# Scores in three rounded passes, and five pieces of work moved between points, in a 1-core fp32 layer stack

## The reference, cut to what matters

```python
# first layer: attention of each head, q and k 64 wide
s = jnp.einsum('bdhnqe,bdhnke->bdhnqk', qb, kb)      # three dilations, masked
...
y_att = o_att * jax.nn.silu(ag.astype(f32))
y = jnp.concatenate([y_att, y_hg], axis=-1).astype(h.dtype) @ w_out
h = h + rmsnorm(y, g_post)
gate = jax.nn.sigmoid((h @ w_pg).astype(f32))
...
# layers two and three: differential attention, two 64-wide halves of a head
qb = lax.dynamic_slice_in_dim(q, i * Q_BLOCK, Q_BLOCK, axis=1)
s = jnp.einsum('bqhcd,bkhcd->bhcqk', qb, k).astype(jnp.float32)
s = jnp.where(kpos[None, :] <= qpos[:, None], s, -jnp.inf)
p = jax.nn.softmax(s, axis=-1)
w = p[:, :, 0] - lam * p[:, :, 1]
...
ret_out = rms_norm(ro).reshape(B, S, RET_W) * jax.nn.silu(rg)
```

## Time and profile before

| | us |
|---|---|
| median of 3 runs | 3032.59 (3032.46 to 3035.77) |
| the profiled execution | 3033.25 |
| its span in the trace | 3031.2 |
| PE busy | 2968.0 (98%) |
| DVE, ACT, POOL busy | 1616.7, 1304.1, 1351.8 |
| mean granted PE clock | 0.994 |

### The profile page before, as it was taken

The page is one execution under the profiler, slowest core; times in us unless marked ns, Lnnn a source line. Parts: engine busy times, 40 slices in busy tenths (PEclk is TensorE's granted clock), DMA queues, the critical chain, the costliest instruction groups (busy, mean ns, idle before and its releaser), DMA issues. The chain is left out here.

```text
span 3031.2 us, 48608 instructions
## 1 busy us (share of the span) xinstructions
PE 2968.0 (98%) x17338; PEld 2407.8 (79%) x17338; DVE 1616.7 (53%) x2411; ACT 1304.1 (43%) x2552; POOL 1351.8 (45%) x1022
## 2 busy tenths in 40 slices
PE   8999999999999999999999999999999999999998
PEld 6888888877777788878888877788888888777886
DVE  5377666655657306653556575551435565755412
ACT  6545444354556334453333334453533333344532
POOL 4444444443433356454444433344644444433444
PEclk9999999999999999999999999999999999999999
DMA  6322222222222334333322222243343222222433
GB/s 240 107 86 108 83 83 82 72 84 83 81 77 78 131 119 153 104 118 136 118 91 87 91 84 70 77 147 102 121 149 118 91 86 92 84 70 74 149 101 107
DMA packets 79010, 313.30 MB, mean 103 GB/s; under 512 B 7440, under 2 KB 11920, under 8 KB 51472
## 3 DMA queue, kind: packets, MB, share of 16 engines
q1 hardware_dynamic: 54832, 266.62, 26.1%
q10 hardware_dynamic: 24032, 44.76, 4.2%
HBM read 293.01 MB, written 18.35 MB: 103 GB/s over the span
## 5 line engine op out<-in xcount | busy, mean ns | idle before, releaser
L340 POOL TENSOR_TENSOR w_low<-w_raw,w_high 128x512 fp32r<-128x512 f32 x844 | 1136.1, 1351 | 1525.2 <-ACT w_high L851 1502.5
L405 PE MATMUL z<-u_high,w_high 128*128 128x512 f32 x3216 | 1277.4, 397 | 15.3 <-DVE work L1491 14.6
L406 PE MATMUL z<-u_low,w_high 128*128 128x512 f32 x3216 | 1257.9, 391 | 0.0
L851 ACT ACTIVATE w_high<-w_raw 128x512 fp32r<-128x512 f32 x832 | 520.0, 629 | 1112.6 <-PE z L409 1075.9
L409 PE MATMUL z<-u_high,w_low 128*128 128x512 f32 x3216 | 862.3, 390 | 0.0
L405 PEld LDWEIGHTS z<-u_high,w_high 128*128 128x128 f32 x3216 | 605.8, 188 | 165.2 <-issue 32.4
L409 PEld LDWEIGHTS z<-u_high,w_low 128*128 128x128 f32 x3216 | 605.0, 188 | 127.7
L406 PEld LDWEIGHTS z<-u_low,w_high 128*128 128x128 f32 x3216 | 606.3, 189 | 119.7
L1867 DVE TENSOR_TENSOR work<-work 128x512 f32<-128x512 f32 x78 | 90.9, 1165 | 277.5 <-ACT work L1140 264.8
L1491 DVE TENSOR_TENSOR work<-z,work 128x512 f32<-128x512 f32 x110 | 76.1, 692 | 181.9 <-PE z L409 145.3
L363 POOL TENSOR_TENSOR pass_weights<-w_raw,pass_weights 128x512 fp32r<-128x512 f32 x96 | 134.4, 1424 | 62.3 <-ACT pass_weights L1053 61.8
(11 more groups left out here) (341 smaller groups left out, 3698.3 us busy)
## 6 DMA issues: line engine op xcount, KB each, us to landing
w_raw<-in_wt SPq DMA_DIRECT2D x213, 1024.0 KB, 4.9
w_raw<-in_wt SPq DMA_DIRECT2D x144, 256.0 KB, 3.0
out_hT<-work ACTq DMA_DIRECT2D x10, 1024.0 KB, 5.8
work<-out_hT ACTq DMA_DIRECT2D x8, 1024.0 KB, 10.3
work<-in_xT SPq DMA_DIRECT2D x4, 1024.0 KB, 16.5
e_scratch<-work ACTq DMA_DIRECT2D x1, 4096.0 KB, 16.7
work<-in_xT ACTq DMA_DIRECT2D x4, 1024.0 KB, 10.9
mixed<-e_scratch ACTq DMA_DIRECT2D x4, 1024.0 KB, 9.2
```

Source lines behind the costliest of these rows:

```text
L340: pool.tensor_tensor(WL[:, 4 * q:4 * q + 4, :], RAW[:, t.odd, 512 * q:512 * q + 512].rearrange("p (k c) -> p k c", k=4), WH[:, 4 * q:4 * q ...
L405: pe.matmul(bank[:], WH[:, k, :], UH[:, k, :], start=(k == 0), stop=False)
L406: pe.matmul(bank[:], WH[:, k, :], UL[:, k, :], start=False, stop=False)
L851: act.activation(WH[:, 4 * q:4 * q + 4, :], RAW[:, n.odd, 512 * q:512 * q + 512].rearrange("p (k c) -> p k c", k=4), ACT.Copy).then_inc(se ...
```

## The change

1. **Scores.** A head's score matmul becomes three fp32r matmuls (`head_scores`): high by high, high by low, low by high, the two heads in turn. `take_heads` makes the parts: two rounded copies (heads_high, QKH), a drain, and two subtractions (heads_low, QKL).
2. **Rotation.** In the differential steps the first rotation goes from point 6 to point 7, behind `dif_out`.
3. **Roots.** `root_row` and `turn_back` come one region later, and between the first and second layer one (first half) or three (second half) regions later.
4. **Gate tile.** In the R_DIF step the gate's `rstd_mul` and `bounded` are taken at point 11 and only the product at the end; the RG-LRU gate's `rstd_mul` and `bounded` follow right behind the step, its product at point 3 of the next.
5. **Third tile.** After pair step 13 PE runs three quarters of the third output tile (`third_ahead`), ahead of `att_values`. They signal `third_used`, on which ACT waits before it rounds three quarters of the next tile's weights into the same place; the fourth quarter stays in `third_tiles` and frees four at once.

```diff
-            def quarter(t, q, gen=None, spare=None, behind=2):
+            def quarter(t, q, gen=None, spare=None, behind=2, done="w_free", freed=1):
...
-                mm.then_inc(sem("w_free"), 1)
+                mm.then_inc(sem(done), freed)
...
-            def third_tiles(t):
+            def third_tiles(t, ahead=0):
                 for s in range(2):
-                    for q in range(4):
-                        quarter(t.plus(2 + s), q, spare=None if s else OUT_BANK)
+                    for q in range(0 if s else ahead, 4):
+                        quarter(t.plus(2 + s), q, spare=None if s else OUT_BANK, freed=ahead + 1 if ahead and not s else 1)
+            def third_ahead(t, n):
+                pe.wait_ge(sem("sm_done"), PRIMED + 8 * PAIRS)
+                for q in range(n):
+                    quarter(t.plus(2), q, spare=OUT_BANK, done="third_used")
...
+            def head_scores(n, hd, a, w):
+                o = slice(64 * hd, 64 * hd + 64)
+                q, k = ((QKH, QKH), (QKH, QKL), (QKL, QKH))[n]
+                return pe.matmul(SC[hd][:, 0:w], q[o, 0, a * P:(a + 1) * P], k[o, 1, 0:w], start=(n == 0), stop=(n == 2))
...
             def dif_scores(j, a):
-                for hd in range(2):
-                    u = 2 * a + hd
-                    pe.wait_ge(sem("dsm_done"), PRIMED + j * 8 + max(u - 1, 0))
-                    o, w = 64 * hd, (a + 1) * P
-                    pe.matmul(SC[hd][:, 0:w], row(QT)[o:o + 64, a * P:(a + 1) * P], row(KTR)[o:o + 64, 0:w],
-                              start=True, stop=True).then_inc(sem("ds_done"), 1)
+                w = (a + 1) * P
+                for n in range(3):
+                    for hd in range(2):
+                        if n == 0:
+                            pe.wait_ge(sem("dsm_done"), PRIMED + j * 8 + max(2 * a + hd - 1, 0))
+                        mm = head_scores(n, hd, a, w)
+                        if n == 2:
+                            mm.then_inc(sem("ds_done"), 1)
...
                 if pg:
-                    return {6: lambda: root_row(n),
-                            7: lambda: turn_back(n, (sem("pg_prod"), 14 + 2 * h), h, (0, 12), BACK_PG[h])}
-                return {3: lambda: root_row(n),
-                        4: lambda: turn_back(n, (sem("z_free"), t - T_HGG + (5 if h else 2)), h, (12,), BACK)}
+                    return {7 + 2 * h: lambda: root_row(n),
+                            8 + 2 * h: lambda: turn_back(n, (sem("pg_prod"), 14 + 2 * h), h, (0, 12), BACK_PG[h])}
+                return {4: lambda: root_row(n),
+                        5: lambda: turn_back(n, (sem("z_free"), t - T_HGG + (5 if h else 2)), h, (12,), BACK)}
...
                     for q in range(4 if weights else 0):
-                        if region is None:
+                        if ahead and q < 3:
+                            high(tt, q, q + 1, "third_used")
+                        elif region is None:
                             high(tt, q)
...
             def take_heads(done):
                 v.drain()
-                v.tensor_copy(row(QT), row(QN))
-                v.tensor_copy(row(KTR), row(KN)).then_inc(sem(done), 1)
+                for n, x in ((0, QN), (1, KN)):
+                    v.tensor_copy(QKH[:, n, :], row(x))
+                v.drain()
+                for n, x in ((0, QN), (1, KN)):
+                    i = v.tensor_tensor(QKL[:, n, :], row(x), QKH[:, n, :].bitcast(F32), ALU.subtract)
+                i.then_inc(sem(done), 1)
...
-                dif = dict(rot=(CTD, STD, 32), scales=scd, take="dqt_ready", ends=(6, 10), gate_tile_at=2)
+                dif = dict(rot=(CTD, STD, 32), scales=scd, take="dqt_ready", ends=(7, 10), gate_tile_at=2)
                 step(Tile(T_L2 + R_DIF, (PER_LAYER, l)), gate=(gl + 6, 6), work="ret", j=l * RET_HEADS + RET_HEADS - 1, m=5,
-                     **{**dif, "ends": (3, 7)})
+                     **{**dif, "ends": (3, 7), "gate_taken_at": 11})
+                rstd_mul(Tile(T_L2 + R_DIF + 3, (PER_LAYER, l)), row(RW))
+                bounded()
```

More of the change, by code:

```diff
@@ L757, in _, with last_pair @@
                 step(Tile(T_ATT, (4, i)), work="att", j=i - 1, late=i - 2)
-            step(None, work="att", j=PAIRS - 1, late=PAIRS - 2, at=LAST_PAIR, between={p: lambda p=p: pair_step(Tile(T_OUT), p - 1, 1) for p in range(1, 16)})
+            def last_pair(p):
+                pair_step(Tile(T_OUT), p - 1, 1)
+                if p == 14:
+                    third_ahead(Tile(T_OUT), 3)
+            step(None, work="att", j=PAIRS - 1, late=PAIRS - 2, at=LAST_PAIR, between={p: lambda p=p: last_pair(p) for p in range(1, 16)})
             pair_step(Tile(T_OUT), 15, 1)
-            third_tiles(Tile(T_OUT))
+            third_tiles(Tile(T_OUT), 3)
             def tiles_in_pairs(t, a, b):
@@ L1129, in out_slots, with one @@
             def out_slots(t, n, gain, block, loads, region):
-                def one(tt, m, s, used, bank, weights=True, taken=None, region=None):
+                def one(tt, m, s, used, bank, weights=True, taken=None, region=None, ahead=False):
                     for q in range(4 if weights else 0):
-                        if region is None:
+                        if ahead and q < 3:
+                            high(tt, q, q + 1, "third_used")
+                        elif region is None:
                             high(tt, q)
@@ L1146, in out_slots @@
                 for s in range(2):
-                    one(t.plus(2 + s), 2 + s, s, n + s + 1, Z[s] if s else OUT_BANK)
+                    one(t.plus(2 + s), 2 + s, s, n + s + 1, Z[s] if s else OUT_BANK, ahead=block == 1 and s == 0)
                 with act.Fori(2, OUT_FULL // 2 - 1) as i:
@@ L1791, in step @@
                             rstd_mul(t.plus(3), row(VT))
+                    if p == gate_taken_at:
+                        rstd_mul(t.plus(gate_tile_at), row(RW))
+                        bounded()
                     if work is not None:
@@ L1822, in step @@
                         else:
-                            gate_tile(t.plus(gate_tile_at), gate[0], MIX[:, gate[1], :])
+                            if gate_taken_at is None:
+                                rstd_mul(t.plus(gate_tile_at), row(RW))
+                                bounded()
+                            gate_product(gate[0], MIX[:, gate[1], :])
             def hg_col(i):
@@ L1828, in lru_gate, with lru_product @@
             def lru_gate(t, n, b):
-                gate_tile(t, n, row(RW))
+                rstd_mul(t, row(RW))
+                bounded()
+                lru_product(n, b)
+            def lru_product(n, b):
+                gate_product(n, row(RW))
                 v.tensor_tensor(MIX[:, 10 + b, :], MIX[:, 10 + b, :], row(RW), ALU.mult).then_inc(sem("lru_done"), 1)
```

18 lines of the change are left out of this document (10 added, 8 removed).

## The result

| | us |
|---|---|
| before, median of 5 runs | 3032.59 (3031.93 to 3035.77) |
| changed, median of 5 runs | 3017.33 (3014.90 to 3020.64) |
| ratio, with 95% interval | 0.9948 (0.9933 to 0.9962) |
| changed, profiled execution and its span | 3018.78, 3016.8 |
| forecast | 3008 (3000 to 3023) |

The kernel became faster by 15.3 us, 0.5%. The side and the range were right; the gain is 60% of the 25.2 that the sum had. The runs of the changed kernel also lie further apart (5.7 us) than a forecast of single microseconds would like: the slowest of the five had a mean granted clock of 0.993 and the fastest 0.995, and 0.002 of 3017 us is 6.

The account below looks back on a forecast made before the run. PE, busy 98% of the span, was taken as the bound, with its waits, the half clock behind them and the score blocks as costs. Terms summed to −25.2 from 3033.25, giving 3008 us, range 3000 to 3023.

Parts of the forecast that it names:

- The blocks: Score blocks: three fp32r passes take a 512-column block from 1.06 to 0.87 us; −5.0 attention, −2.2 differential heads.
- the plain sum for the differential turns: Turns between differential heads: DVE's added drain and subtractions, 1.46 us at six turns without cover, +8.7.
- the rotation: Differential heads: the last product moved ahead of the rotation on DVE removes four PE waits of 1.53, −6.1.
- both new waits: PE would newly wait 2.7 us for the heads' copies at the gate, and 2.9 ahead of the third tile's last quarter.
- Rivals 1 and 2: Score blocks: two heads' passes run one after another, 3041, chance 0.12; or each pass waits for its weights, 3021, 0.09.
- Rival 3: DVE's added work at the turns costs its upper ends, +8 differential and +2 attention: 3018, chance 0.08.
- Rival 4: Output part and gate only move their waits, half clock each time, last pair at its upper end: 3014, within the forecast.
- the last pair: Third tile's three quarters replace the wait for the last pair's probabilities; new wait and clock chance included, −2.2 (+1 to −4).
- Rival 5: The turns cost 6 instead of 8.7 and there is no half clock at all: 3002, an edge of the forecast.
- the likeliest case: Whole kernel: all terms as summed, 3008, with 3001 to 3015 as edges; chance 0.68.
- Each added microsecond is a wait there: Turns of the differential heads: without cover, DVE's added time becomes PE waiting, 6 × 1.46 = +8.7.
- the 2.99 wait goes whole behind three steps: Token scale, second half: three steps of PE work (4.08 us) hide the wait, −2.99, and its half clock, −1.7.

Follow-up runs that it names:

- the shifted run: Changed kernel with 96 more, already met semaphore waits at the start of PE's program, moving all later instructions in its stream; one run, 3021.22 us.

## Why the prediction came out as it did

**What held.** The blocks (0.90 against 0.87), the two heads side by side, the plain sum for the differential turns (+8.6 against +8.7), the rotation, and both new waits in kind and nearly in size (2.06 for 2.7 at the gate, 2.85 for 2.9 ahead of the last quarter). Rivals 1 and 2 fell: the blocks of both orders take 0.90. Rival 3's 3018 is the measured number by chance only: it had the turns at their upper end, and they cost their plain sum. Rival 4 had the half clock right: in the profiled execution it came behind both gate waits and the last quarter's. Its 3014 doesn't hold the last pair's upper end that it names; with that it is 3015. Rival 5 fell too, since the turns cost 8.6 and lost clock besides. The range held although the sum was 9 us off and the median lies outside the likeliest case's 3001 to 3015; that it was wide enough owes to rivals 2 and 3, which didn't happen.

**The clock.** The step that failed is in the part on the three passes: "Each added microsecond is a wait there", and no more than a wait. The gate and the last pair were given a chance of half clock, the turns none, and no reason is given. Three turns lost 4.8 us in the profiled execution, and both gate waits lost theirs where a quarter of a chance was taken. Over six kernels it was a quarter of the turns and three quarters of the gate waits. The run that fills the waits gives the whole of it, −7.0 between the profiled executions. Which of the turns lose it changes from trace to trace (in the run with the token scale moved back, the second turn lost it and the first didn't). That this is why the runs of this kernel spread fits with their granted clocks, but only one of the five was traced.

**The roots.** The step "the 2.99 wait goes whole behind three steps" failed. PE did run three steps in its place, but DVE's chain, which had been 12.4, became 15.1, with five of DVE's ten updates beside GpSimd's subtractions instead of one. A wait of 1.76 stayed: −3.5 for −6.1. The prediction named nothing that could grow there. That the new order of PE's work is what put them side by side is argued from the start times, which moved by 5 us, and not shown apart.

**What wasn't in the sum.** The waits put down to issue in the attention values, +3.9 with the clock behind the first. The prediction counted the added matmuls' time and not their place: twenty more PE records ahead (five blocks with two more matmuls and two more loads each) moved the wait twenty records forward in the code, and it grew. The trace of the run with three passes in the attention pairs alone shows it, and the shifted run shows that it hangs on the place in the stream; why it is longer there stays open.

**The last pair** was 1.6 for 2.2, since the low clock behind the new wait came whole (3.4 us at 0.51) where 1.0 was set.

## What to carry to other kernels

Price a wait of the bounding engine twice, for its length and for the chance of a low clock behind it (here a quarter at 1.55 to 1.91 us, three quarters at 2.06); where the wait can't go, filling it with idle matmuls can pay by itself (some 7 us here). Before three cheaper passes replace one, ask what must be made ready for them and whether that has cover where the operands turn: with 2.6 us of it the subtractions were free, with none they cost more than the passes gave, and keeping one old matmul at the head of each group bought the cover in six of eight heads. When a wait goes, look at which engine's work now lies beside which: the same ten operations took 5.1 or 9.3 us.

## What the runs showed of the hardware that was not expected

- Two heads' matmuls on separate halves of the rows ran side by side in either program order: with two matmuls between them in the program their first passes started 10 ns apart.
- A wait of 1.55 was followed by a stretch at 1.2 GHz (0.53 of full clock over 3.4 us) in some places of one execution, and in others of another kernel's, 9 of 36 turns over six kernels.
- In the first run through a stretch of 256 matmuls at 14 ns each, PE waited 1.4 to 2.9 us for nothing that the profile shows, at a fixed count of its records, and 20 more records ahead moved it to other matmuls. The loop's later rounds had no such wait.
- A 256-column DVE update with two inputs took 1.5 instead of 0.47 us beside a GpSimd subtraction.
